# In the four norms of a two-block transformer step, tile evictions and splits are interleaved with the rows of the next tiles

## What is computed

```python
# first block
xn = rms_norm(h, ln1_w)                  # first norm
h = h + mix(xn @ w_in) @ w_out
hn = rms_norm(h, ln2_w)                  # second norm
h = h + square(relu(hn @ w_up)) @ w_down
# second block
h = standardize(x) * (1 + sc1) + sh1     # third norm
x = layer_norm(ALPHA * x + (1 + g1) * mixer(h), ln1_gain, ln1_bias)
h = standardize(x) * (1 + sc2) + sh2     # fourth norm
```

## Time and profile before

| | us |
|---|---|
| median of three runs | 1685.16 |
| lowest and highest | 1680.59, 1685.27 |
| the profiled execution | 1684.55 |
| its span (first to last instruction) | 1682.7 |

### The profile page before, as it was taken

The page is one execution under the profiler, slowest core; times in us unless marked ns, Lnnn a source line. Parts: engine busy times, 40 slices in busy tenths (PEclk is TensorE's granted clock), DMA queues, the critical chain, the costliest instruction groups (busy, mean ns, idle before and its releaser), DMA issues. The chain is left out here.

```text
span 1682.7 us, 19667 instructions
## 1 busy us (share of the span) xinstructions
PE 1528.8 (91%) x7216; PEld 1227.6 (73%) x7216; DVE 879.9 (52%) x1492; ACT 592.2 (35%) x864; POOL 645.4 (38%) x456
## 2 busy tenths in 40 slices
PE   4999989797999999997998999979993999999995
PEld 3776855576888788875878777768882888888884
DVE  4672378625868776497281454425647332333337
ACT  4322377015222121216251464433427332232232
POOL 2332300033646555463451322235631444544441
PEclk7999979898999999997997998989995999999998
DMA  7222100043645555212541632243321222223221
GB/s 277 81 89 80 34 17 2 1 163 122 213 170 204 185 178 185 100 50 88 137 149 69 181 101 100 93 150 122 117 76 75 76 100 101 90 88 113 86 100 50
DMA packets 48182, 185.72 MB, mean 110 GB/s; under 512 B 12960, under 2 KB 14112, under 8 KB 33248
## 3 DMA queue, kind: packets, MB, share of 16 engines
q1 hardware_dynamic: 30240, 165.53, 27.7%
q10 hardware_dynamic: 17856, 19.01, 4.1%
HBM read 169.71 MB, written 12.58 MB: 108 GB/s over the span
## 5 line engine op out<-in xcount | busy, mean ns | idle before, releaser
L1413 POOL TENSOR_TENSOR wlo<-raw,whi 128x512 fp32r<-128x512 f32 x448 | 639.7, 1459 | 1003.0 <-ACT whi L898 1002.9
L441 PE MATMUL bank<-Ahi,whi 128*128 128x512 f32 x1088 | 440.5, 405 | 22.1 <-issue 8.5
L442 PE MATMUL bank<-Alo,whi 128*128 128x512 f32 x1088 | 431.8, 397 | 0.0
L443 PE MATMUL bank<-Ahi,wlo 128*128 128x512 f32 x1088 | 430.9, 396 | 0.0
L898 ACT ACTIVATE whi<-raw 128x2048 fp32r<-128x2048 f32 x113 | 216.4, 1915 | 280.6 <-PE bank L471 216.9
L441 PEld LDWEIGHTS bank<-Ahi,whi 128*128 128x128 f32 x1088 | 209.7, 193 | 71.6 <-issue 17.4
L442 PEld LDWEIGHTS bank<-Alo,whi 128*128 128x128 f32 x1088 | 209.5, 193 | 44.8 <-issue 2.4
L443 PEld LDWEIGHTS bank<-Ahi,wlo 128*128 128x128 f32 x1088 | 209.2, 192 | 45.3
L469 PE MATMUL bank<-whi,Bhi 128*128 128x512 f32 x496 | 195.4, 394 | 5.7 <-POOL wlo L1413 5.7
L471 PE MATMUL bank<-whi,Blo 128*128 128x512 f32 x496 | 194.3, 392 | 0.0
L470 PE MATMUL bank<-wlo,Bhi 128*128 128x512 f32 x496 | 194.2, 391 | 0.0
(11 more groups left out here) (381 smaller groups left out, 1941.5 us busy)
## 6 DMA issues: line engine op xcount, KB each, us to landing
raw<-in_ws SPq DMA_DIRECT2D x113, 1024.0 KB, 4.9
adaw<-in_ada SPq DMA_DIRECT2D x48, 512.0 KB, 4.8
spill<-stage ACTq DMA_DIRECT2D x32, 256.0 KB, 2.0
X<-in_x SPq DMA_DIRECT2D x8, 512.0 KB, 5.8
gates<-spill SPq DMA_DIRECT2D x16, 256.0 KB, 2.9
w1k<-in_w1k SPq DMA_DIRECT2D x1, 2048.0 KB, 15.4
w1v<-in_w1v SPq DMA_DIRECT2D x1, 2048.0 KB, 19.7
XM<-spill ACTq DMA_DIRECT2D x8, 256.0 KB, 3.6
```

The source lines that it names most:

```text
L441: pe.matmul(ps[:], wh, hi[:, k], start=(k == 0), stop=False)
L442: pe.matmul(ps[:], wh, lo[:, k], start=False, stop=False)
L443: ins = pe.matmul(ps[:], wl, hi[:, k], start=False, stop=(k == kn - 1))
L1413: pool.tensor_tensor(wlo[slot][:, part], raw[slot][:, part], rd(whi[slot][:, part]), ALU.subtract).then_inc(sem("lo_split"), 1)
```

## The change

No instruction is added or taken away. Four sequences are put into another order:
- ACT, norms 0 to 2: from row 1 on, `scaled` of tile i-1 follows row i, the last tile's comes at the end. In the first norm the next weight tile's high part now follows row 2; in the others it still follows row 1, ahead of `scaled(0)`.
- ACT, fourth norm: `scaled` of tiles 0 and 1 follows the steps of i = 2 and i = 3.
- DVE: in the first and fourth norm `parts` of tiles 0 and 1 follows the steps of rows 2 and 3; in the second and third `parts` of tile 0 follows row 1's scale, and the other three stay at the end.
- PE: the transposes of tile 0 in the second and third norm stand ahead of the last but one run.

```diff
                 for q, i in ((0, 0), (0, 1), (0, 2), (1, 0), (0, 3), (1, 1), (1, 2), (1, 3)):
                     run(q, i)
-                    if turns and (q, i) == (1, 2):
+                    if turns and (q, i) == (1, 1):
                         normed_tile(s, 0)
...
                     normed_row(i, s)
                     if i == 1 and s:
                         hi_upto(more)
-                if s == 0:
-                    hi_upto(more)
-                    act.wait_ge(sem("par_in"), A.due("par_in", 16))
-                elif s == 2:
-                    act.wait_ge(sem("mod_ready"), A.due("mod_ready"))
-                for i in range(NT):
-                    scaled(i, s)
+                    if i == 1 and s == 0:
+                        act.wait_ge(sem("par_in"), A.due("par_in", 16))
+                    if i == 1 and s == 2:
+                        act.wait_ge(sem("mod_ready"), A.due("mod_ready"))
+                    if i == 2 and s == 0:
+                        hi_upto(more)
+                    if i:
+                        scaled(i - 1, s)
+                scaled(NT - 1, s)
...
                 if i:
                     normed_row(i - 1, 3)
+                if i >= 2:
+                    scaled(i - 2, 3)
             spread_of(NT - 1)
             normed_row(NT - 1, 3)
-            for i in range(NT):
+            for i in range(NT - 2, NT):
                 scaled(i, 3)
...
                 row_scale(i, True)
+                if i >= 2:
+                    parts(0, i - 2)
             dve.wait_ge(sem("par_in"), v.due("par_in", 16))
-            for i in range(NT):
+            for i in range(NT - 2, NT):
                 parts(0, i)
...
                     row_scale(i, s < 2)
-                for i in range(NT):
+                    if i == 1:
+                        parts(s, 0)
+                for i in range(1, NT):
                     parts(s, i)
...
                 if i:
                     again_scale(i - 1)
+                if i >= 2:
+                    parts(3, i - 2)
             again(NT - 1)
             dve.sem_inc(sem("gb_used"), 1)
             again_scale(NT - 1)
-            for i in range(NT):
+            for i in range(NT - 2, NT):
                 parts(3, i)
```

## The result

The kernel with the change takes 1696.91 us (median of 4 runs, 1695.37 to 1699.52), the kernel before beside it 1683.82 us (1680.59 to 1685.27). The ratio is 1.0071 with a 95% interval of 1.0055 to 1.0086: 0.7% slower. In us the interval is 9.3 to 14.5, and the two medians lie 13.1 apart. The profiled execution of after took 1697.33 us, its span is 1695.5 us, 12.8 more than before's 1682.7.

A forecast was written before the change was run, and what follows sets the result against it. PE is busy 1528.8 of 1682.7 us, so time is won or lost where it waits in the norms' engine-changing chains. Norms one to four: -2.7 + 3.85 + 4.85 + 4.7 = +10.7 us, giving 1695 us, range 1686 to 1701.

The forecast's parts named there:

- The chain: Norms two to four: rows wait behind tile 0's parts, outweighing shorter tails; +3.85, +4.85 and +4.7 us.
- The exclusion of DVE and POOL: Second and third norm: tile 0's casts and subtractions alternate with POOL's operations, taking 1.37 and 1.64 us, not 0.43 and 0.69.
- the two bounds: Norm losses with full DVE and POOL exclusion and with none: second +3.85 or +0.35, third +4.85 or +1.85 us.
- The upper bound: Loss with full DVE and POOL exclusion: +3.85 us in the second norm, +4.85 in the third.
- The lower: Loss without any DVE and POOL overlap: +0.35 us in the second norm, +1.85 in the third.
- The first norm's bound without overlap: First norm: product 5.1 us earlier if DVE's parts don't meet POOL, against 2.7 earlier with overlap.
- No overlap cost: Rival, all norms: POOL's operations fall elsewhere or DVE wins; +1.8 us, 1686.4, no measurable change; chance 0.11.
- The interleaving works as written: Rival, all norms: rows come as early as before and tails lose four halves; 1665.5 us, faster; chance 0.05.
- Partly absorbed: Rival, downstream of the norms: waits not hanging on the product's start absorb half the loss; +5 us, 1690; chance 0.08.
- The larger loss: Rival: lower clock after PE's gaps, PE's stall reaching row 2, or longer POOL holds; 1 to 2 us a norm, 1700; 0.11.
- the distances between norms: Stretches from one norm's product to the next norm: predicted unchanged by the change.
- the clock of the first products: PE's products behind each norm: predicted to add nothing, since PE comes from similar low-clock stretches in both kernels.

The follow-up runs named there:

- the four kernels of one norm each: The kernel before with only one norm's part of the change: first 1680.29, second 1687.93, third 1691.93, fourth 1690.01 us; before took 1685.38.
- the last version: Against before: first norm as changed, whi earlier in second and third, tile 0's eviction in ACT's gaps in second and fourth; 1675.51 us, ratio 0.9942.

## Why the prediction was right, step by step

For each norm I take the start of row 1's addition as common to both traces, so the times of after are shifted by 1.14 us in the second norm, 6.55 in the third and 9.34 in the fourth.

| step | said | measured |
|---|---|---|
| second norm: tile 0 done | 393.3 | 392.8 |
| row 2 normed | 395.9 | 395.3 |
| row 3 normed | 399.75 | 399.0 |
| product | 405.7 | 405.3 |
| third norm: row 2's addition | 769.8 | 769.4 |
| row 3 normed | 777.1 | 776.6 |
| product | 784.1 | 783.7 |
| fourth norm: first cast | 1278.9 | 1278.9 |
| row 3's addition later by | 5.7 | 5.7 |
| last gain step later by | 10.4 | 10.5 |
| product | 1306.0 | 1306.1 |

**The chain.** The step on which all rests held: DVE's program names tile 0's parts ahead of row 2, ACT's order puts the eviction behind row 1 and whi, so a row that was ready waits for one that isn't. The 4.11 us in the bracket of the cast are that wait. What it pays back is fewer evictions behind the last row: from the start of the last normed row to the product it was 6.24 us in after's second norm (400.17 to 406.41) against 11.02 in before (390.83 to 401.85). These 4.8 us did not make up for the row being 8.2 later (forecast 8.9).

**The exclusion of DVE and POOL.** Both 1.37 and 1.63 us were as forecast from the earlier trace rows, and the kernel with POOL held back shows that POOL is the cause. By the rule of the Trainium skill ("SBUF — State Buffer", section "Who interferes with whom") these pairs exclude each other for a whole instruction; the runs agree, 1.63 beside POOL and 0.69 without. The size is less certain than the two bounds made it look: they lie 3.5 us apart in the second norm (+3.85 against +0.35), and holding POOL back gave 2.1. The upper bound was 0.4 too high, summed over a whole chain of small steps. The lower was not tested as it stands, because with POOL held back the same work meets row 2's var step and costs 0.8 there: the norm lost 1.3, and less 0.8 that is 0.5 against 0.35. So the bound's "no overlap" describes neither kernel. In the third norm the bounds were 1.85 and 4.85, measured 2.0 and 4.5. The first norm's bound without overlap (-5.1) has no working in the prediction, and no kernel tested it.

**No overlap cost** (1686.4) was the rival to the forecast, and the kernel with POOL held back is nearly that case in the second and third norm: +1.3 and +2.0 there, 1689.41 in all. The stretched operations of after had ruled it out before that. **The interleaving works as written** fell by row 2's addition at 393.94. **Partly absorbed** fell: in the four kernels of one norm each, nothing of a norm's loss comes back in another norm, and as the medians lie 13.1 us apart, half of the norms' 9.5 did not come back between them either. **The larger loss** had 1700 by longer gaps of PE; the norms gave 9.5 of the 10.7 that I forecast, and the 1.2 less is made up by -3.2 in place of -2.7 in the first norm, and by 0.4 each that I took too much in the second and third. With the same start the first norm's product would stand at 28.30 against my 28.75: DVE and ACT were some 0.5 earlier throughout (POOL at 17.57 with that start, forecast 17.7; tile 1's first cast at 20.03, forecast 20.5).

**What was wrong.** I wrote that the distances between norms would be unchanged. In the sum they were 2.8 longer, but the true failure is that I took one trace's distance for a property of the kernel; it varies by 5.0 us between two executions of one program. The median fell near the forecast of 1695 (1696.9), with the norms giving a little less than I said and the rest of the difference more; that the two partly cancel is luck. I also wrote that the clock of the first products adds nothing. Behind the first norm PE's steps shorten from 0.43 to 0.23 us 6.1 us after the first product in before and 2.7 in after. Over all traces it is 4.0 to 6.1 with the old first norm (five traces) and 2.7 to 6.1 with the new (eight). An estimate from the steps: 3.4 us longer at 0.43 a product in place of 0.23 cost 1.6 us. So there is a term of up to that size that I had left out, and whether its mean depends on the change stays open.

## What to carry to other kernels

Engines run their lists in order, so a step that is moved forward must be ready when the one it displaces is; otherwise it delays work that was ready, and it has done so even where the busy times are the same. Look at which gaps the profile shows ahead of the moved step, and put it into the gap (in the last version, ACT's gap between rows 2 and 3) rather than into the list. And where a step starts another engine's work, here whi that starts POOL, place that work too: it cost 2.1 and 2.4 us where it met the moved steps, and moving whi alone to an earlier place gained 1.0 us in the third norm without any interleaving. When a gain is measured from an event inside the norm, look whether the change also delays that event: 0.7 us were hidden there.

## What the runs showed of the hardware

A 128x1 operation of DVE with two inputs (var) lasts 0.22 us alone and took 0.98 to 1.27 beside POOL's subtractions (1.27 in row 3 of before's own second norm), though it has one element a partition; its like in the third norm (nmr, 0.16 alone) took 0.42 to 0.88. A BATCH_NORM_STATS2 of 128x512 and the addition of a bank to X, 0.69 each, kept their length in the same stretches. So the delay goes by the kind of the operation and not by its size; it was at most 1.05 us, and one of POOL's subtractions lasts about 1.24 (4.94 for four). In the kernel with whi behind the eviction:

```profile
386.47 4.94 POOL L1417 TENSOR_TENSOR wlo<-raw,whi 128x512 fp32r<-128x512 f32 x4 [16.95 <-ACT whi L898]
...
386.76 0.69 DVE L1437 BATCH_NORM_STATS2 st<-X 128x6 f32<-128x512 f32 x1
...
387.73 1.24 DVE L1446 SCALAR_TENSOR_TENSOR var<-mv 128x1 f32<-128x1 f32 x1
```

The other thing is how much of an execution's time is not set by the program. The norms, in which the engines wait for each other, repeat to 0.03 us; the long stretches of products, in which PE is nearly always busy, differ by up to 5 us between two executions of one program. In the one stretch looked into, PE's granted clock was 0.97 in one and 0.91 in the other. A difference of 2 or 3 us there, read from one trace each, says nothing.
